# One gather for both expert tables in a hybrid decoder step: 8 KB rows, eight places, weights made column by column

## The chip, the cores and the metric

One core of one Trainium2 chip runs the whole program. The metric is the device time in microseconds. The kernel before took 2368.91 us, the median of three runs (2366.36 to 2372.15). Engines are named as in the profile: PE is TensorE (PEld its weight loads), DVE VectorE, ACT ScalarE, POOL GpSimd, SP SyncE; a "q" behind a name is the engine's sequencer.

## The reference

One layer of a decoder, for 512 prompt tokens and 8 x 8 sample tokens with a paged past of 2048. Two attention mixers (one over selected keys, one over a compressed latent) are projected and added to x; then comes the part that the change touches, a feed-forward layer of 16384 single-neuron experts, of which each token takes 16 for each of 8 heads:

```python
# PEER, for a block of 128 tokens xb (normalised)
q = (xb @ w_peer_q).reshape(128, 8, 2, 64)
s = einsum('thpd,hpnd->thpn', q, peer_sub_keys)       # two halves, 128 keys each
sv, si = top_k(s, 16)
cand = sv[:, :, 0, :, None] + sv[:, :, 1, None, :]    # 256 pairs per head
cv, ci = top_k(cand, 16)                              # e: the expert of each pair
g = softmax(cv)
act = gelu(einsum('td,thkd->thk', xb, peer_u[e]))
y = einsum('thk,thkd->td', g * act, peer_v[e])        # added to x1
```

Both tables, peer_u and peer_v, are 16384 x 1024 in float32: one row is 4 KB.

## The kernel before

The program has one long prelude (to about 441 us: projections of five tiles of 128 tokens, prompt attention, routing of the first tile) and then a loop of steps (line 1072 on ACT, 1679 on DVE, 2217 on PE). All engines run the same steps by number, each in its own instruction stream, tied only by semaphores.

A column is one expert for each of 128 tokens, one token per partition. There are 128 columns for each of four prompt tiles and 64 for the sample tile, 576 in all. POOL gathers a column's rows by an indirect DMA with 128 indices (line 682): one from peer_u and one from peer_v, 512 KB each. The row of peer_u for column k is fetched for step k; that of peer_v for step k + LAG with LAG = 22. A ring of 16 places of 4 KB per partition takes both kinds in the order of use, and now and then a chunk of query weights or output weights ("w", "o"). POOL fills a place when the one who used it last is done: the dot for a row of peer_u, the transposes or the addition for a row of peer_v, the matmuls for a weight chunk.

At step k DVE multiplies the landed row of peer_u by the token's vector h (kept in PSUM, h_now) and sums it into acts[column] (line 1690, the dot). After 16 columns ACT applies gelu to all 16 sums (line 1078) and DVE multiplies by the gates into wts (line 1706). The row of peer_v is taken in one of two ways, by the list SHARES (line 342), which names for stretches of steps the share that goes to DVE: either ACT scales the row by its weight in place (line 1086) and PE one step later adds it to accT in PSUM by eight transposes against the identity (line 2230); or DVE multiplies and adds it into xall (line 1701). The sample tile's columns all go the first way. When a tile is over, ACT copies the sums out of PSUM and PE turns them back.

Between these column parts each engine's step has other parts, put down by a plan of first and last step and a count of marks (lines 362 to 389): eight batches of latent attention (b0 to b7, 55 steps each from step 36), the indexer's scores (idx, 100 to 160), the search for the selected keys by 32 trials (top, 166 to 351), eight batches of attention over selected keys (a0 to a7, from 361), the routing of the next tile (r1 to r4: norm, query matmuls, key scores) and the choice of its experts (c1 to c4), and the second half of the first tile's choice (c0b, 0 to 36). The pages of the caches are gathered on the same POOL queue (line 623), at places in the order of fetches that AHEAD sets. The norm of tile t puts its row into hbuf (line 1236), from which PE turns it and DVE copies it to h_now. mix_rest (line 1407) adds the output projection of the last two prompt tiles at step MIXED_AT = LAG; PE's first transposes and the first latent batch wait for it. Eight of the 16 places are the space of w_out and come free as the projection uses it.

## Time and profile before

| what | value |
|---|---|
| median of three runs | 2368.91 us (2366.36 to 2372.15) |
| span of the profiled execution | 2346.3 us (22.6 us below the median; its own total time isn't shown) |
| PE, PEld busy | 1763.5 us (75%), 1299.5 us (55%) |
| DVE busy | 1610.7 us (69%) |
| ACT busy | 989.6 us (42%) |
| POOL busy | 1234.0 us (53%) |
| HBM read, written | 690.14 MB, 3.76 MB |
| gathers of peer_u, peer_v (line 682) | 576, 576 |
| granted PE clock, mean | 0.807 |

The span is the time from the first to the last instruction of one profiled execution. Busy shares are averages over all stages. Issue time of a DMA on POOL counts as busy; the transfer does not. A wait names the engine whose semaphore came last by the profile; "issue" means that nothing in the profile explains the pause, and "another core or an unknown queue" (in the waits: remote) an event without an engine.

### The profile page before, as it was taken

The page shows a single profiled execution, that of the slowest core. Times are in us where ns is not written, and L with a number is a line of the kernel's source. Part 1 is how long each engine was busy: PE and PEld are TensorE (multiplying, and loading weights), DVE is VectorE, ACT ScalarE, POOL GpSimd, SP SyncE. Part 2 cuts the span into 40 slices and gives each one's busy share as a digit, 9 for nine tenths or more (in the row PEclk, how much of TensorE's full clock was granted, in tenths as well). Part 3 has the DMA queues.
Part 4 walks back from the last instruction along what each step waited for, and adds up shares of the span by engine and source line. Part 5 has one row for each costly group of instructions (what it writes and reads, how often), then busy time and mean ns, then how long its engine had stood idle before and what let it go on. Part 6 is the DMA issues. An engine that isn't in the chain of part 4 may idle for free.

```text
span 2346.3 us, 26214 instructions
## 1 busy us (share of the span) xinstructions
PE 1763.5 (75%) x8918; PEld 1299.5 (55%) x8918; DVE 1610.7 (69%) x3641; ACT 989.6 (42%) x1711; POOL 1234.0 (53%) x1251
## 2 busy tenths in 40 slices
PE   7995999638858967987877977847876976753556
PEld 3553657327646756665655755636654655543445
DVE  2546682887876777778676786786887778677441
ACT  1223343133544323555665664643342443233345
POOL 1000000367666666666667666656566656767664
PEclk9997799858977857978978987977987887875667
DMA  7001202499998989999999999979899889999997
GB/s 256 24 11 38 56 1 73 156 354 405 351 342 331 346 312 353 354 359 370 344 361 392 372 354 385 344 262 389 314 354 376 314 325 348 373 401 348 358 372 283
DMA packets 191573, 695.64 MB, mean 296 GB/s; under 512 B 26192, under 2 KB 28624, under 8 KB 188368
## 3 DMA queue, kind: packets, MB, share of 16 engines
q0 software_dynamic: 178608, 674.33, 76.2%
q1 hardware_dynamic: 12832, 19.65, 2.8%
q8 instruction: 70, 1.15, 0.2%
q14 instruction: 63, 0.52, 0.1%
HBM read 690.14 MB, written 3.76 MB: 296 GB/s over the span
## 4 chain that ended last, share of the span: by engine, by line
PE 42%; DVE 21%; issue 12%; POOL 6%; ACT 6%; another core or an unknown queue 5%; DVEq 4%; DMA 4%; ACTq 0%; POOLq 0%
PE ps L2230 8%; PE ps L2037 7%; DVE region L1690 6%; POOL region L682 6%; DVEq L1097 4%; DVE xall L1701 3%; DMA region<-in_peer_v,region 3%; PE ps L1722 2%; ACT region L1086 2%; PE ps L2054 2%; PE ps L1987 2%; PE ps L2130 1%; PE ps L2019 1%; PE ps L2082 1%
## 5 line engine op out<-in xcount | busy, mean ns | idle before, releaser
L682 POOL DMA_INDIRECT region<-in_peer_u,region x507 | 515.7, 1017 | 611.6 <-DVEq L1097 440.1
L2230 PE MATMUL ps<-ident,region 128*128 128x128 f32 x3312 | 552.7, 325 | 262.4 <-issue 138.1
L682 POOL DMA_INDIRECT region<-in_peer_v,region x571 | 571.7, 1001 | 335.2 <-issue 145.8
L1690 DVE SCALAR_TENSOR_TENSOR region<-region,h_now 128x1024 f32<-128x1024 f32 x507 | 611.7, 1214 | 116.5 <-DMA region<-in_peer_u,region 69.6
L2230 PEld LDWEIGHTS ps<-ident,region 128*128 128x128 f32 x3312 | 472.1, 169 | 350.6 <-issue 204.3
L1086 ACT ACTIVATE region<-region 128x1024 f32<-128x1024 f32 x414 | 464.9, 1139 | 245.0 <-DMA region<-in_peer_v,region 189.0
L2037 PE MATMUL ps<-w_uk_s,region 128*128 128x512 f32 x544 | 294.3, 669 | 8.7 <-issue 6.7
L1701 DVE SCALAR_TENSOR_TENSOR xall<-region,xall 128x1024 f32<-128x1024 f32 x157 | 201.7, 1285 | 20.9 <-issue 4.7
L2037 PEld LDWEIGHTS ps<-w_uk_s,region 128*128 128x128 f32 x544 | 106.3, 218 | 91.8 <-issue 88.2
L946 ACT ACTIVATE region<-ps 128x512 f32<-128x512 f32 x136 | 80.2, 590 | 163.5 <-PE ps L2037 101.3
L953 ACT ACTIVATE region<-ps 128x256 f32<-128x256 f32 x136 | 51.5, 379 | 202.2 <-remote 115.0
L1428 DVE TENSOR_REDUCE region<-region 128x8 f32<-128x512 f32 x136 | 92.6, 681 | 62.4 <-issue 41.2
L1690 DVE SCALAR_TENSOR_TENSOR tables<-tables,h_now 128x1024 f32<-128x1024 f32 x69 | 83.9, 1216 | 21.6 <-DMA tables<-in_peer_u,region 16.6
L682 POOL DMA_INDIRECT tables<-in_peer_u,region x69 | 70.8, 1026 | 29.6 <-issue 18.9
L2017 PE MATMUL ps<-region 128*128 128x64 f32 x272 | 52.5, 278 | 43.1 <-issue 29.2
L2017 PEld LDWEIGHTS ps<-region 128*128 128x128 f32 x272 | 47.4, 209 | 67.3 <-issue 50.1
L2054 PE MATMUL ps<-region 128*64 128x256 f32 x272 | 72.9, 424 | 8.9 <-issue 4.7
L2130 PE MATMUL ps<-region 128*128 128x64 f32 x272 | 51.2, 346 | 37.4 <-ACT region L1033 20.9
L2130 PEld LDWEIGHTS ps<-region 128*128 128x128 f32 x272 | 47.1, 256 | 50.6 <-issue 25.3
L1722 PE MATMUL ps<-region 128*128 128x512 f32 (+1 forms) x192 | 69.3, 515 | 5.5 <-ACT region L703 5.5
L864 ACT ACTIVATE region<-region,stat 128x128 f32<-128x128 f32 (+3 forms) x64 | 35.9, 561 | 81.5 <-DVE stat L1368 81.4
L1003 ACT ACTIVATE region<-region 64x2056 bf16<-64x2056 f32 x32 | 63.8, 1994 | 0.0
(404 smaller groups left out, 2824.5 us busy)
## 6 DMA issues: line engine op xcount, KB each, us to landing
region<-in_w_peer_q POOLq DMA_DIRECT2D x31, 512.0 KB
region<-in_peer_v,region POOLq DMA_INDIRECT x571
region<-in_peer_u,region POOLq DMA_INDIRECT x507
region<-in_w_in POOLq DMA_DIRECT2D x8, 882.0 KB, 14.8
region<-in_w_peer_q SPq DMA_DIRECT2D x8, 512.0 KB, 4.7
region<-in_x_turned SPq DMA_DIRECT2D x5, 512.0 KB, 3.5
region<-in_w_out SPq DMA_DIRECT2D x2, 1024.0 KB, 12.4
region<-in_w_out SPq DMA_DIRECT2D x1, 2048.0 KB, 18.3
```

What stands on the lines that cost most here:

```text
L682: pool.indirect_dma_start(ring[r][:], None, table, bass.IndirectOffsetOnAxis(ap=experts[:, t, n:n + 1], axis=0)).then_inc(landed[r], 16)
L1086: sc(ring[r][:], ring[r][:], ACT.Copy, scale=wts[:, t % 2, n:n + 1]).then_inc(S["v_scaled"], 1)
L1097: dve.drain()
L1428: v.tensor_reduce(norm_s[:, q - 3, :], sq_s[:, n % 2, :].rearrange("p (h d) -> p h d", h=HB), AX, ALU.add).then_inc(S["reduced"], 1)
L1690: v.scalar_tensor_tensor(ring[r][:], ring[r][:], 1.0, h_now[:], ALU.mult, ALU.mult, accum_out=acts[:, t % 2, n:n + 1]).then_inc(S["u_done" ...
L1701: v.scalar_tensor_tensor(xall[:, t, :], ring[r][:], wts[:, t % 2, n:n + 1], xall[:, t, :], ALU.mult, ALU.add).then_inc(S["v_mixed"], 1)
L1722: last = te.matmul(ps[2 + i][:, 0:w], xT[:, t % 2, c, :], w_in[:, c, c0:c0 + w], start=(c == 0), stop=(c == KD - 1))
L2017: te.matmul(dst, cT_s[:, m % 2, 0, :], qabs[:, 0, :, cols], start=True, stop=False)
L2037: last = te.matmul(ps[2][:], cT_s[:, m % 2, c, :], w_uk[:, c, :], start=(c == 0), stop=(c == 1))
L2054: te.matmul(ps[2][0:NTOK, 0:DC], s_s[:, g, :], c_s[:, g, :], start=(g == 0), stop=(g == NPG))
L2130: last = te.matmul(ps[5][:, g % 8 * NTOK:(g % 8 + 1) * NTOK], kT_s[:, (q - 1) % 2, g - g0, :], q_blk[:], start=True, stop=True)
L2230: last = te.matmul(ps[6 + c // 4][:, (c % 4) * P:(c % 4 + 1) * P], ring[r][:, c * P:(c + 1) * P], ident[:], is_transpose=True, start=(m == ...
```

## The change

The host lays both tables side by side as one array peer_rows of 16384 x 2048, so that an expert's rows are one row of 8 KB. One gather per column brings it. The ring has eight places of 8 KB: three in the space of the former first six, four in that of w_out, and the last over hbuf and the space behind it, free after the first dot. The normalised row of tiles 1 to 4 therefore goes to tables (h_rows) instead of hbuf. Two weight chunks share a place. The lag of 22 steps goes: at step k DVE does the dot of column k; ACT, for column k - 1, applies gelu to the one sum, multiplies by the gate with a copy, and scales the second half of the row where PE takes it; DVE's addition is for column k - 1 and waits for ACT's weight; PE's transposes are for column k - 2. A place is free when the row has been added. The first columns (steps below 6) and the first four columns of tiles 1 to 3 go to DVE; the list's last entry goes. MIXED_AT is 6. Per column ACT gets two small activations and one or two drains; the grouped gelu on ACT and the grouped product on DVE go.

```diff
-        ring = [Region(X_END + r * D, KEPT_END).view(D) for r in range(EXTRA)]
-        ring.append(tables[:, 0:D])
-        ring.append(Region(HBUF_AT + D, SIZE).view(D))
-        ring += [Region(W_OUT_PLACE + c * D, W_OUT_PLACE + KD * D).view(D) for c in range(KD)]
-        W_OUT_AT = EXTRA + 2
+        W = 2 * D
+        ring = [Region(X_END + r * W, X_END + EXTRA * D).view(W) for r in range(EXTRA // 2)]
+        W_OUT_AT = len(ring)
+        ring += [Region(W_OUT_PLACE + c * W, W_OUT_PLACE + KD * D).view(W) for c in range(KD // 2)]
+        HBUF_SLOT = len(ring)
+        ring.append(Region(HBUF_AT, SIZE).view(W))
+        h_rows = [hbuf] + [tables[:, 0:D]] * (NTILE - 1)
...
-        LAG = 22
-        GRP = 16
+        ADD_LAG, PE_LAG = 1, 2
-        SHARES = [(38, 54, 3, 4), (100, 160, 2, 3), (167, 184, 1, 2), (258, 275, 1, 2), (362, 480, 3, 5), (480, 496, 1, 2), (SEQ, STEPS, 1, 2)]
+        MIXED_AT = 6
+        SHARES = [(0, MIXED_AT, 1, 1), (38, 54, 3, 4), (100, 160, 2, 3), (167, 184, 1, 2), (258, 275, 1, 2), (362, 480, 3, 5), (480, 496, 1, 2)]
+        HEAD = 4
         def on_dve(m):
-            k = m + LAG
+            if P <= m < SEQ and m % P < HEAD:
+                return True
+            k = m + ADD_LAG
...
-        AHEAD = NRING // 2 - 1
+        AHEAD = NRING - 1
...
-            if k < NCOLS:
-                fetched.append(("u", *tile_of(k)))
-            if k >= LAG:
-                fetched.append(("v", *tile_of(k - LAG)))
+            fetched.append(("e", *tile_of(k)))
...
-                    if kind_ == "u":
-                        pool.wait_ge(S["u_done"], x + 1)
-                    elif kind_ != "v":
+                    if kind_ != "e":
                         pool.wait_ge(S["w_used"], weights_used(fetched[f - NRING]))
                     elif on_dve(x):
                         pool.wait_ge(S["v_mixed"], x - pe_rows(x) + 1)
                     else:
                         pool.wait_ge(S["v_added"], pe_rows(x) + 1)
+                elif f == HBUF_SLOT:
+                    pool.wait_ge(S["dotted"], 1)
                 elif f >= W_OUT_AT:
-                    pool.wait_ge(S["o_up"], 4 + f - W_OUT_AT + 1)
+                    pool.wait_ge(S["o_up"], 4 + 2 * (f - W_OUT_AT) + 2)
...
-                    table = a["peer_u"] if kind == "u" else a["peer_v"]
-                    pool.indirect_dma_start(ring[r][:], None, table, ...)
+                    pool.indirect_dma_start(ring[r][:], None, a["peer_rows"], ...)
...
-                if k % GRP == 1 and 1 < k <= NCOLS + 1:
-                    j = k // GRP - 1
-                    act.wait_ge(S["dotted"], j + 1)
-                    t, n = tile_of(GRP * j)
-                    sc(acts[:, t % 2, n:n + GRP], acts[:, t % 2, n:n + GRP], ACT.Gelu_apprx_tanh).then_inc(S["gelu"], 1)
+                m = k - ADD_LAG
                 if 0 <= m < NCOLS:
-                    if m % GRP == 0:
-                        act.wait_ge(S["wts"], m // GRP + 1)
+                    act_, weight = acts[:, t % 2, n:n + 1], wts[:, t % 2, n:n + 1]
+                    act.wait_ge(S["dotted"], m + 1)
+                    sc(act_, act_, ACT.Gelu_apprx_tanh)
+                    act.drain()
+                    sc(weight, act_, ACT.Copy, scale=gates[:, t, n:n + 1]).then_inc(S["wts"], 1)
                     if not on_dve(m):
-                        act.wait_ge(landed[r], landing["v", t, n])
-                        sc(ring[r][:], ring[r][:], ACT.Copy, scale=wts[:, t % 2, n:n + 1]).then_inc(S["v_scaled"], 1)
+                        act.drain()
+                        sc(ring[r][:, D:W], ring[r][:, D:W], ACT.Copy, scale=weight).then_inc(S["v_scaled"], 1)
...
-                    v.scalar_tensor_tensor(ring[r][:], ring[r][:], 1.0, h_now[:], ALU.mult, ALU.mult,
-                                           accum_out=acts[:, t % 2, n:n + 1]).then_inc(S["u_done"], 1)
-                    if k % GRP == GRP - 1:
-                        settle()
-                        dve.sem_inc(S["dotted"], 1)
-                m = k - LAG
+                    v.scalar_tensor_tensor(ring[r][:, 0:D], ring[r][:, 0:D], 1.0, h_now[:], ALU.mult, ALU.mult,
+                                           accum_out=acts[:, t % 2, n:n + 1]).then_inc(S["dotted"], 1)
+                m = k - ADD_LAG
                 if 0 <= m < NCOLS and on_dve(m):
-                    dve.wait_ge(landed[r], landing["v", t, n])
+                    dve.wait_ge(S["wts"], m + 1)
                     settle()
-                    v.scalar_tensor_tensor(xall[:, t, :], ring[r][:], wts[...], xall[:, t, :], ALU.mult, ALU.add).then_inc(S["v_mixed"], 1)
-                if k % GRP == 2 and 2 < k <= NCOLS + 2:
-                    dve.wait_ge(S["gelu"], j + 1)
-                    v.tensor_tensor(wts[:, t % 2, n:n + GRP], acts[:, t % 2, n:n + GRP], gates[:, t, n:n + GRP], ALU.mult).then_inc(S["wts"], 1)
+                    v.scalar_tensor_tensor(xall[:, t, :], ring[r][:, D:W], wts[...], xall[:, t, :], ALU.mult, ALU.add).then_inc(S["v_mixed"], 1)
...
-                m = k - LAG - 1
+                m = k - PE_LAG
```

## Rows read from the trace of the kernel before

**Rows 1.** Busy us (instructions) by stretch, granted PE clock, DMA share, GB/s
```profile
441.00:586.00 145.00, 91.36 (x455) 67.01 (x454) 114.60 (x265) 42.48 (x71) 99.21 (x103) 0.77 0.95 368
586.00:735.00 149.00, 109.15 (x567) 79.88 (x568) 116.19 (x337) 72.36 (x108) 95.27 (x98) 0.80 0.95 355
735.00:952.00 217.00, 177.71 (x898) 136.02 (x898) 159.93 (x223) 73.52 (x159) 138.62 (x134) 0.74 0.90 328
952.00:1541.00 589.00, 476.43 (x2670) 358.32 (x2668) 433.99 (x1076) 362.01 (x552) 387.56 (x400) 0.87 0.97 364
1541.00:2006.00 465.00, 340.91 (x1786) 260.61 (x1786) 361.05 (x498) 166.26 (x312) 290.73 (x278) 0.78 0.88 333
2006.00:2124.00 118.00, 74.35 (x415) 61.50 (x413) 86.21 (x213) 42.89 (x54) 78.15 (x84) 0.77 0.97 377
2124.00:2346.00 222.00, 115.91 (x618) 96.93 (x616) 95.36 (x150) 88.71 (x83) 137.69 (x144) 0.65 0.92 349
```

**Rows 2.** Timeline of POOL in the end stretch: start us, us, instruction, idle before
```profile
2223.30 0.94 POOL L682 DMA_INDIRECT region<-in_peer_v,region  x1 [0.30 <-issue]
```

**Rows 3.** Stretches of line 1690 (twice), line 1086, line 1701 alone
```profile
586.00:2124.00 1538.00, 554.42 (x916) 0.81 0.93 350
952.00:1541.00 589.00, 231.37 (x382) 0.87 0.97 364
...
586.00:2124.00 1538.00, 359.98 (x322) 0.81 0.93 350
...
586.00:2124.00 1538.00, 174.75 (x136) 0.81 0.93 350
```

**Rows 4.** Stretches as in rows 1, with 4 KB rows, then 8 KB rows
```profile
2222.00:2232.00 10.00, 6.28 (x25) 5.07 (x26) 4.92 (x8) 4.29 (x5) 6.56 (x7) 0.50 1.03 413
1697.50:1699.50 2.00, 2.00 (x16) 1.60 (x14) 2.00 (x3) 0.94 (x3) 1.70 (x2) 1.00 0.98 399
```

**Rows 5.** Chain of waits by line, of 586 to 2124, then 2124 to 2346
```profile
by line: issue 13.2%; PE ps L2037 10.3%; PE ps L2230 9.8%; DVE region L1690 7.2%; another core or an unknown queue 5.3%; DVEq L1097 4.5%; DVE xall L1701 3.9%; PE ps L2054 3.2%; ACT region L1086 3.1%; DMA region<-in_peer_v,region 2.7%; PE ps
by line: POOL region L682 43.3%; issue 19.7%; PE ps L2230 14.1%; another core or an unknown queue 8.5%; DMA region<-in_peer_v,region 4.8%; POOL tables L682 3.0%; DVE region L1690 1.1%; ACT region L1086 1.0%; DVE xall L1701 0.6%; DVE h_now L
```

**Rows 6.** Waits of 586 to 2124: us in total, times, longest
```profile
ACT region L1086 <- DMA region<-in_peer_v,region: 80.3, 30, 9.0
POOL region L682 <- remote: 79.5, 45, 3.8
PEld ps L2230 <- ACT region L1086: 77.1, 50, 16.1
POOL region L682 <- PE ps L2230: 76.9, 45, 4.7
```

**Rows 7.** Line 623, gathers of 8 KB rows: ns min/median/max, first and last start
```profile
L623 POOL DMA_INDIRECT region<-in_cache_a_v,page_idx x8: 932/936/1790, 1583.5 to 1951.8; - x8
```

**Rows 8.** Timeline of DVE (last dot) and of PE at the end
```profile
2299.95 1.22 DVE L1690 SCALAR_TENSOR_TENSOR region<-region,h_now 128x1024 f32<-128x1024 f32 x1 [1.32 <-DMA region<-in_peer_u,region]
...
2337.42 1.04 PE L2230 MATMUL ps<-ident,region 128*128 128x128 f32 x8
```

**Rows 9.** Timeline of DVE at the first landed row
```profile
446.05 1.23 DVE L1688 COPY h_now<-region 128x1024 f32<-128x1024 f32 x1 [4.05 <-DMA region<-in_peer_u,region]
```

**Rows 10.** Groups of instructions on ACT: busy us, mean ns
```profile
L836 ACT ACTIVATE stat<-stat 128x1 f32<-128x1 f32 x5 | 1.0, 203 | 0.1
```

**Rows 11.** Timeline of ACT around a grouped gelu
```profile
1313.63 1.28 ACT L1078 ACT_TABLE_LOAD   x1
1314.93 0.22 ACT L1078 ACTIVATE region<-region 128x16 f32<-128x16 f32 x1
1315.05 1.13 ACT L1086 ACTIVATE region<-region 128x1024 f32<-128x1024 f32 x1
```

**Rows 12.** Groups of table loads on ACT, first and last of six lines
```profile
L1078 ACT ACT_TABLE_LOAD x24 | 30.8, 1283 | 0.4
...
L932 ACT ACT_TABLE_LOAD x5 | 6.4, 1283 | 0.1
```

More of the change, by code:

```diff
@@ L364, in program @@
         C_PAGES = [(0, 6), (6, 12), (12, NPG + 1)]
-        chain_b = [(f"b{b}", 36 + 55 * b, 36 + 55 * b + 50, MB) for b in range(NB)]
-        MIXED_AT = LAG
+        B_AT = 36
+        chain_b = [(f"b{b}", B_AT + 55 * b, B_AT + 55 * b + 50, MB) for b in range(NB)]
         NBIT = 31
@@ L399, in program @@
             for c, k in enumerate(marks(f"r{t}", 6, KD)):
-                weights[k].append(("w", t, c))
+                if c % 2 == 0:
+                    weights[k].append(("w", t, c))
         for c, k in enumerate(marks("mixS", 0, KD)):
-            weights[k].append(("o", NTILE - 1, c))
-        AHEAD = NRING // 2 - 1
+            if c % 2 == 0:
+                weights[k].append(("o", NTILE - 1, c))
+        AHEAD = NRING - 1
         pages = [[] for _ in range(STEPS)]
-        pages[MIXED_AT + AHEAD].append(("b", 0))
+        pages[B_AT - NRING + AHEAD].append(("b", 0))
         pages[88].extend((("i", 0), ("i", 1)))
@@ L415, in program @@
         fetched, beside = [], {}
-        for k in range(NCOLS + LAG):
+        for k in range(NCOLS):
             beside[len(fetched)] = pages[k]
             fetched += weights[k]
-            if k < NCOLS:
-                fetched.append(("u", *tile_of(k)))
-            if k >= LAG:
-                fetched.append(("v", *tile_of(k - LAG)))
-        assert sum(len(x) for x in weights[NCOLS + LAG:] + pages[NCOLS + LAG:]) == 0
+            fetched.append(("e", *tile_of(k)))
+        assert sum(len(x) for x in weights[NCOLS:] + pages[NCOLS:]) == 0
         place_of, landing, count = {}, {}, [0] * NRING
@@ L426, in program @@
             r = f % NRING
[L427 removed]
+            count[r] += 2 * KVA * 16 if what[0] == "o" and what[2] < G else 16
             place_of[what], landing[what] = r, count[r]
         def weights_used(what):
[L432 removed]
+            return KD * ((NTILE if what[1] == NTILE - 1 and what[0] == "w" else what[1])) + what[2] + 2
         def advance(k, parts):
@@ L1983, in route @@
                 for c in range(KD):
-                    r = place_of["w", t, c]
-                    pe.wait_ge(landed[r], landing["w", t, c])
+                    r = place_of["w", t, c // 2 * 2]
+                    pe.wait_ge(landed[r], landing["w", t, c // 2 * 2])
                     for h in range(PH):
-                        last = te.matmul(ps[3 + 2 * (h // 4)][:, (h % 4) * P:(h % 4 + 1) * P], ring[r][:, h * P:(h + 1) * P], h2T[:, c, :],
+                        last = te.matmul(ps[3 + 2 * (h // 4)][:, (h % 4) * P:(h % 4 + 1) * P], ring[r][:, c % 2 * D + h * P:c % 2 * D + (h + 1) * P], h2T[:, c, :],
                                          start=(c == 0 and h % 4 == 0), stop=(c == KD - 1), skip_group_check=True)
@@ L2181, in mix_sample @@
                 for c in range(KD):
-                    r = place_of["o", NTILE - 1, c]
-                    pe.wait_ge(landed[r], landing["o", NTILE - 1, c])
+                    r = place_of["o", NTILE - 1, c // 2 * 2]
+                    pe.wait_ge(landed[r], landing["o", NTILE - 1, c // 2 * 2])
                     for j, bank in enumerate((3, 5)):
-                        last = te.matmul(ps[bank][:], oT_s[:, c, :], ring[r][:, 512 * j:512 * j + 512], start=(c == 0), stop=(c == KD - 1))
+                        x = c % 2 * D + 512 * j
+                        last = te.matmul(ps[bank][:], oT_s[:, c, :], ring[r][:, x:x + 512], start=(c == 0), stop=(c == KD - 1))
                     last.then_inc(S["w_used"], 1)
@@ L2281 @@
     for name in _INS:
-        arrays[name] = _np.ascontiguousarray(inputs[name])
+        if name not in ("peer_u", "peer_v"):
+            arrays[name] = _np.ascontiguousarray(inputs[name])
+    arrays["peer_rows"] = _np.concatenate([inputs["peer_u"], inputs["peer_v"]], axis=1)
     arrays["page_table"] = _np.ascontiguousarray(_np.repeat(arrays["page_table"].T, P // NPG, axis=0))
```

51 lines of the change are left out of this document (25 added, 26 removed).

## Prediction

> **What bounds the kernel now.** I read the stretches of the span first, then the chain of waits, then the waits themselves. The rows of experts are fetched from 441 us to the end, 1905 of the 2346.3 us. [rows 1] cuts that into the start (441 to 586), five stretches that I call the middle (586 to 2124, in which other work goes with the columns: sample attention, routing, the top-key search), and the end (2124 to 2346, hardly anything but columns). The reader should see that no engine is full in the middle. Summed over its five rows PE is busy 1178 of 1538 us (77%), DVE 1157 (75%), ACT 717 (47%), POOL 990 (64%). But POOL's 994 instructions each stand 0.30 us apart although nothing holds them [rows 2], so its queue is occupied 990 + 298 = 1288 us, 84%. The DMA engines show 0.93 [rows 3], and moved 350 GB/s there; with nothing in the way they reached 413 in [rows 4], so bytes alone want 350/413 = 85% of the middle. So five resources stand at 75 to 85%, and the loss is in waiting for one another.
>
> The chain of waits says who waits last [rows 5]. In the end stretch it is POOL issue: 43.3 + 3.0% on line 682. Two gathers a column at 0.94 + 0.30 us [rows 2] are 2.49 us, beside 1.049 MB at 413 GB/s = 2.54 us of transfer: two bounds of one size, so that after any hiccup neither can catch up, and 64 columns took 222 us with their tail. In the middle the chain is PE first, then DVE; landings (DMA 2.7%, unknown queue 5.3%, which I read as gathers landing, the only work I know without an engine's name) are 8% of 1538 = 123 us. The waits agree: ACT's scaling waited 80 us for rows of the second table, POOL 80 + 77 us for free places [rows 6].
>
> **The change part by part.** Sums are against the profiled execution, whose own total time is not shown; its span is 2346.3 us, 22.6 under the median of 2368.91. I take that as constant and state differences.
>
> *Half the gathers, rows twice as long.* 1152 gathers become 576. A gather with 8 KB rows already stands in the trace (the value cache) and costs POOL a median 0.936 us [rows 7], as one of 4 KB does. POOL's load per column falls from 2.49 to 1.24 us. The bytes stay. A burst of 8 KB rows ran 399 GB/s at a DMA share of 0.98, 4 KB rows 413 at 1.03 [rows 4]: 407 against 401 per unit of share. I take the rate per byte as equal (2.54 us a column); bounds are 2.50 and 2.63 (1.049 MB at 399).
>
> *End, without the lag of 22.* 64 columns at 2.6 us (2.54 and little for stalls) are 166 us. After the last landing come one dot (554.4/458 = 1.21 us [rows 3]), gelu and weight (0.6, below), scaling (1.12 [rows 3]), eight transposes (1.04), and then what follows them today, from 2338.5 to 2346.3 [rows 8]: 12 us. 178 against 222: **-44**. Bounds -50 (2.5 us a column) and -20 (2.97, 353 GB/s, near the middle's rate).
>
> *Start, without the lag.* The first 54 columns now need both tables' rows, where before the second ran 22 columns behind. 54 x 1.049 + 4.2 (query weights) + 2.4 MB (pages) = 63.2 MB at 413 GB/s = 153 us, and 4 us until the first landing [rows 9]: 157, and 3 more because only three places are free at once and four await the output projection. 160 against 145: **+15**. Bounds +5 (routing work hidden less now) and +27 (at the start's 368 GB/s it would be 172).
>
> *Middle, relief.* POOL at half load refills a stall at twice the transfer's rate. Of the 123 us of landings on the chain I take 60%, since PE, DVE or ACT is next to be late: **-75**. Bounds 0 (others are late at once) and -151 (all of it and some 28 us of POOL issue that lies in shorter stretches of the same chain).
>
> *Middle, ScalarE's load.* Instead of one gelu over 16 columns there is, in every column, a gelu of 128x1, a drain, a copy with a pointer scale, and for PE columns a second drain before the scaling. The nearest row, an activation of 128x1, takes 203 ns [rows 10]; the copy I put at 0.25. Today the scaling starts 0.12 us after a gelu of 0.22 began [rows 11], an overlap of 0.10 that two drains take away: 0.20 + 0.25 + 2 x 0.10 = 0.65, less the share of the old gelu (0.22/16), say 0.6 us a column. Bounds 0.45 and 0.9. ACT goes from 362 to 362 + 0.6 x 191 columns [rows 3] = 477 of 589 us (81%) in the stretch 952 to 1541, from 61%: it becomes as full as PE. Where PE sat waiting for a scaling, 50 times in the middle [rows 6], I add the 0.6 in full: **+30**. Bounds 0 and 193 (all 322 scaled columns [rows 3]).
>
> *Middle, VectorE's addition.* An addition (136 in the middle [rows 3]) waited only for a landed row; now it waits for ACT's weight of the column before. ACT sits first behind its own parts of the step before, which wait for PE. The dot of 1.21 us in front covers 0.6 us if ACT is free. Behind the waiting addition stand DVE's parts and the next dot, and behind those PE. I take 0.25 us each, +34; bounds 0 and 136 x 0.8 = 109 (a square of 0.6 and a copy left over on ACT). The additions themselves go from 159 to 157 by the shares: nothing.
>
> *Table loads.* Gelu, Exp and Sqrt take each other's table out. 24 loads for gelu and 32 for the others (8 + 8 + 6 + 5 + 5, of six lines the first and the last in [rows 12]) stand in the trace, of which all but one or two are in this phase. Afterwards each of the 33 Exp and Sqrt there (two for each of eight latent-attention batches, one for each of eight selected-key batches, four norms, five gates) has one before and one after: at most 66, some 12 more x 1.283 = 15 us of ACT, a third of it on the path: **+5**, bounds 0 and 15.
> The trace has ACT going on 0.02 us after a load ended [rows 11]. The Trainium skill (ScalarE: Activation LUTs, What ACT_TABLE_LOAD costs) says that a switch also drains for about 1.38 us, 2.66 in total, and speaks against a gelu in every column. By it the 12 would cost 32 us of ACT and the term would be +11; by the row it is +5, and no row here shows that drain.
>
> *Places.* Eight places of 8 KB hold as many columns as sixteen of 4 KB. A row now keeps its place through dot, gelu, scaling and transposes, about 5 us or 1.5 steps longer than the first table's did. About 5 columns (13 us of transfer) stay ahead. I cost that at nothing while stalls are under 13 us; the page gathers profit a little, as POOL comes to them later and waits less.
>
> Sum: -44 + 15 - 75 + 30 + 34 + 5 = **-35 us, 2334 us**.
>
> **The rivals.** *B, supply was the bound all along.* For it: POOL 84% and DMA 0.93 in the middle, and 13% of the chain as issue, some of which may be landings. Against: PE and DVE lines lead the chain. All of the 151 goes and the additions' waits shrink to 10: -44 + 15 - 151 + 30 + 10 + 5 = -135, 2234 us.
>
> *C, slower: dot, gelu, scaling and transposes become one chain that every step walks.* Place: ACT in the middle. Price 0.6 us for each column in which ACT is the last. For it: ACT at 81% from 952 to 1541, and DVE, ACT and PE now tied within one or two steps, where today ACT may run ahead of the dots by half a group. Against: today's waits of PE for a scaling are only 50. The rest of the sum is -44 + 15 - 75 + 34 + 5 = -65, so it decides from 65/0.6 = 108 columns on; at 200 of the 322 the time is 2369 - 65 + 120 = 2424 us.
>
> *D, bytes bound it.* The DMA share stays as it is, every added wait hides behind transfer, and the middle does not move. End at its own 373 GB/s (64 columns 180 us, + 12) gives -30, start at 377 (168 + 4) gives +27: 2366 us. For it the share of 0.93 to 0.97; against it 413 GB/s in [rows 4] with 4 KB rows.
> The Trainium skill (DMA: Bandwidth & Descriptors, Specifications) gives an HBM limit of about 358 GB/s per core, by which the middle's 350 would leave nothing to win and D would hold; the trace's 413 over 10 us disagrees, and the measurement decides.
>
> **How the numbers follow.** Forecast A (2300 to 2361) 0.34, B 0.22, C 0.33, D 0.11. No change means within 0.3%, 7 us, about what a measurement of this kernel can tell. Faster: A and B, 0.56; same: D, 0.11; slower: C, 0.33. The range takes in B's middle and C's up to its worked case: 2235 to 2430. A's own is 2300 to 2361.
>
> **What would show it.** POOL busy falls to about 650 us with gathers still at 0.94; if they take 1.5 or more, the first step is wrong. Columns in the end stretch come every 2.5 to 2.6 us. From the start of the last dot to the end of the span it is 12 us, today 46 [rows 8]. ACT's busy time rises by 200 to 300 us. DVE's additions wait for ACT where they waited for nothing. ACT_TABLE_LOADs are 60 to 70. If PE's waits for the scaling line grow from 50 to over 150 and the stretch of the key search is longer than now, C holds. If that stretch shrinks by over 5%, B does. The forecast is wrong in its largest term if the middle still waits for landings as before.

## Result and profile after

The changed kernel takes 2189.18 us (median, 2181.62 to 2195.00), the kernel before beside it 2370.07 (2366.36 to 2372.15): ratio 0.9233 [0.921, 0.9256], 181 us faster. I had forecast 2334 in a range of 2235 to 2430, so the direction was right and the size far off. The nearest rival was B (supply was the bound all along), 2234.

The profiled execution took 2195.0 us with a span of 2193.2. Only 1.8 us lie around the span, so the 22.6 us that I took as constant were no fixed part of a run: the profiled execution of before was itself some 20 us quicker than its median. From trace to trace the gain is 153 us; some 22 of the other 28 are that, and the rest is that this execution of the changed kernel lay 6 us above its median.

Three stretches of the changed kernel, cut at the same columns as in [rows 1] (dots 54 and 512 start at 613 and 2018); columns as there:

```profile
441.00:613.00 172.00, 130.96 (x634) 93.88 (x632) 127.12 (x276) 88.24 (x196) 63.16 (x66) 0.82 0.94 384
613.00:2018.00 1405.00, 1115.97 (x6246) 846.74 (x6246) 1155.80 (x2321) 933.51 (x2068) 508.12 (x516) 0.85 0.96 382
2018.00:2193.00 175.00, 115.02 (x555) 92.95 (x553) 81.91 (x134) 111.09 (x203) 56.26 (x61) 0.65 0.92 379
```

| stretch | before | after | moved | my sum |
|---|---|---|---|---|
| start | 145 (441 to 586) | 172 | +27 | +15 |
| middle | 1538 | 1405 | -133 | -6 (-75 + 30 + 34 + 5) |
| end | 222 | 175 | -47 | -44 |

The middle is where the forecast broke. PE and DVE do the same work there as before, PE for fewer us because its granted clock rose from 0.81 to 0.85 (1116 us against the 1178 summed from [rows 1]). The DMA engines moved 382 GB/s instead of 350, at a share of 0.96 instead of 0.93.

From the changed kernel's page, engine totals and groups (busy us, mean ns, idle time before and who ended most of it):

```profile
PE 1738.6 (79%) x8934; PEld 1272.8 (58%) x8934; DVE 1601.9 (73%) x3603; ACT 1273.8 (58%) x2840; POOL 634.3 (29%) x657
...
q0 software_dynamic: 95376, 674.29, 76.7%
...
L689 POOL DMA_INDIRECT region<-in_peer_rows,region x576 | 567.2, 985 | 1421.5 <-PE ps L2229 752.9
...
L1091 ACT ACTIVATE region<-region 128x1024 f32<-128x1024 f32 x419 | 481.3, 1149 | 34.5 <-issue 0.8
L1086 ACT ACTIVATE region<-region 128x1 f32<-128x1 f32 x576 | 113.2, 196 | 330.3 <-DVE region L1696 322.6
...
L1704 DVE SCALAR_TENSOR_TENSOR xall<-region,xall 128x1024 f32<-128x1024 f32 x157 | 201.8, 1285 | 78.1 <-ACT region L1088 64.0
L1088 ACT ACTIVATE region<-region 128x1 f32<-128x1 f32 x576 | 169.7, 295 | 40.1 <-issue 0.7
```

The reader should see POOL at 634 us (1234 before) with the gather of 8 KB rows at a mean of 985 ns, and on ACT 576 gelus of 0.196 and 576 copies of 0.295 us. ACT's total rose from 989.6 to 1273.8. POOL idles 753 us for PE's transposes: it waits for places, no longer the other way round. The same bytes went in 95,376 packets; the page of before has 178,608.

Waits of the changed kernel in its middle (us in total, times, longest), then its chain of waits by line in the middle and in the end stretch:

```profile
POOL region L689 <- PE ps L2229: 612.3, 255, 19.5
ACT region L1086 <- DVE region L1696: 221.3, 134, 6.1
PEld ps L2229 <- ACT region L1091: 191.5, 134, 7.1
...
DVE region L1696 <- DMA region<-in_peer_rows,region: 78.6, 63, 6.4
...
DVE xall L1704 <- ACT region L1088: 60.7, 35, 5.2
```

```profile
by line: DVE region L1696 12.3%; PE ps L2035 9.0%; PE ps L2229 7.4%; DMA region<-in_peer_rows,region 6.4%; DVE xall L1704 6.0%; ACTq L1087 5.9%; DVEq L1103 4.4%; issue 4.0%; PE ps L1985 3.0%; PE ps L2052 2.7%; ACT region L1091 2.7%; ACT reg
```

```profile
by line: DMA region<-in_peer_rows,region 66.4%; PE ps L2229 8.9%; DVE region L1696 5.7%; ACT region L1091 4.7%; issue 3.7%; POOL region L689 3.2%; ACT region L1088 1.3%; PE ps L2204 1.1%; ACT region L1076 1.0%; ACT region L1086 0.9%; anothe
```

Against [rows 5], "issue" fell from 13.2 to 4.0% and the unknown queue is gone from the front places; the dot, PE's latent attention and the additions lead. Landings are 6.4%, 90 us. PE's weight loads wait for a scaling 134 times (191 us) where [rows 6] has 50 (77 us). In the end stretch landings, 66.4%, have taken POOL's place.

### The profile page after: what moved, and what is told of

It reads as the page before. It is cut to its first block, busy times and chain, and to the rows that moved or that the text cites. A ratio compares the mean times of both kernels' runs of the same rounds, so it can differ in the third digit from the quotient of the medians.

```text
span 2193.2 us, 27671 instructions
## 1 busy us (share of the span) xinstructions
PE 1738.6 (79%) x8934; PEld 1272.8 (58%) x8934; DVE 1601.9 (73%) x3603; ACT 1273.8 (58%) x2840; POOL 634.3 (29%) x657
## 3 DMA queue, kind: packets, MB, share of 16 engines
q0 software_dynamic: 95376, 674.29, 76.7%
## 4 chain that ended last, share of the span: by engine, by line
PE 38%; DVE 28%; DMA 12%; ACT 9%; ACTq 4%; DVEq 4%; issue 4%; POOL 1%; another core or an unknown queue 0%; POOLq 0%
DMA region<-in_peer_rows,region 11%; DVE region L1696 9%; PE ps L2035 6%; PE ps L2229 6%; DVE xall L1704 4%; DVEq L1103 4%; ACTq L1087 4%; PE ps L1985 3%; PE ps L1720 3%; ACT region L1091 2%; PE ps L2052 2%; ACT region L1088 1%; PE ps L2017 1%; PE ps L1888 1%; ACT region L1010 1%
## 5 line engine op out<-in xcount | busy, mean ns | idle before, releaser
L689 POOL DMA_INDIRECT region<-in_peer_rows,region x576 | 567.2, 985 | 1421.5 <-PE ps L2229 752.9
L1696 DVE SCALAR_TENSOR_TENSOR region<-region,h_now 128x1024 f32<-128x1024 f32 x576 | 695.8, 1216 | 203.4 <-DMA region<-in_peer_rows,region 191.1
L2229 PE MATMUL ps<-ident,region 128*128 128x128 f32 x3352 | 567.8, 327 | 248.0 <-ACT region L1091 225.1
L1091 ACT ACTIVATE region<-region 128x1024 f32<-128x1024 f32 x419 | 481.3, 1149 | 34.5 <-issue 0.8
L1086 ACT ACTIVATE region<-region 128x1 f32<-128x1 f32 x576 | 113.2, 196 | 330.3 <-DVE region L1696 322.6
L2035 PE MATMUL ps<-w_uk_s,region 128*128 128x512 f32 x544 | 282.1, 644 | 5.9 <-ACT region L953 5.9
L1088 ACT ACTIVATE region<-region 128x1 f32<-128x1 f32 x576 | 169.7, 295 | 40.1 <-issue 0.7
L1985 PEld LDWEIGHTS ps<-region 128*128 128x128 f32 x512 | 61.3, 197 | 5.6 <-issue 3.8
L1985 PE MATMUL ps<-region 128*128 128x128 f32 x512 | 62.7, 280 | 1.2 <-ACT region L905 1.2
L1947 PE MATMUL ps<-ident,region 128*128 128x128 f32 x160 | 34.4, 318 | 36.6 <-ACT region L871 36.3
L2017 PE MATMUL ps<-region 32*128 32x64 f32 x272 | 61.2, 306 | 0.0
L2015 PEld LDWEIGHTS ps<-region 128*128 128x128 f32 x272 | 46.6, 205 | 24.4 <-issue 13.9
```

The source lines that it names most:

```text
L689: pool.indirect_dma_start(ring[r][:], None, a["peer_rows"], bass.IndirectOffsetOnAxis(ap=experts[:, t, n:n + 1], axis=0)).then_inc(landed[ ...
L1086: sc(act_, act_, ACT.Gelu_apprx_tanh)
L1088: sc(weight, act_, ACT.Copy, scale=gates[:, t, n:n + 1]).then_inc(S["wts"], 1)
L1091: sc(ring[r][:, D:W], ring[r][:, D:W], ACT.Copy, scale=weight).then_inc(S["v_scaled"], 1)
L1696: v.scalar_tensor_tensor(ring[r][:, 0:D], ring[r][:, 0:D], 1.0, h_now[:], ALU.mult, ALU.mult, accum_out=acts[:, t % 2, n:n + 1]).then_inc( ...
L1985: last = te.matmul(ps[3 + 2 * (h // 4)][:, (h % 4) * P:(h % 4 + 1) * P], ring[r][:, c % 2 * D + h * P:c % 2 * D + (h + 1) * P], h2T[:, c, ...
```

## Experiments

All times are medians. Sets of executions on different chips differ for the kernel before (2340 to 2373, and one of 2137, below), hardly for the changed one, so I compare changed kernels with each other, and on one chip where 10 us matter. Kernels with two gathers may move with the chip as the kernel before does, and none was run on two chips, so a difference of 10 us between two of them tells nothing. The changed kernel beside later variants took 2185.45.

> The changed kernel itself, beside the other three on one chip, so that differences of ten microseconds can be told: 2185 to 2195.

Its trace has the first dot at 446 and dot 54 at 604, where the first trace had 455 and 613: 9 of the start's +27 us belong to that one execution.

**Two gathers, everything else changed.** The two tables stay apart, and each column takes two gathers of 4 KB rows into the halves of one place:

```diff
-  pool.indirect_dma_start(ring[r][:], None, a["peer_rows"], ...)
+  for half, table in ((ring[r][:, 0:D], a["peer_u"]), (ring[r][:, D:W], a["peer_v"])):
+      pool.indirect_dma_start(half, None, table, ...)
```

> The changed kernel, with each column's two rows fetched again by two gathers of 4 KB rows from the two tables into the two halves of the same place. Lag, places, gelu per column stay as changed. Theory S (the supply held the middle: two gathers a column on POOL at 1.24 us each and the shorter rows): most of the 181 us come back, 2330 to 2390 us, POOL's queue over 80% occupied again, columns of the end stretch back at 2.5 us or more. Rival L (the gain came from what goes with it: no lag, other shares, places freed otherwise): it stays at 2190 to 2230.

Measured: 2340.98, ratio 0.9939 [0.9901, 0.9977] to before. Its stretches:

```profile
448.00:625.00 177.00, 128.15 (x602) 95.73 (x601) 119.83 (x262) 87.21 (x196) 114.63 (x119) 0.72 0.97 370
625.00:2146.00 1521.00, 1160.07 (x6242) 872.25 (x6241) 1157.68 (x2321) 934.33 (x2068) 979.39 (x971) 0.82 0.95 352
2146.00:2341.00 195.00, 118.71 (x558) 96.99 (x556) 81.88 (x134) 110.57 (x203) 115.80 (x124) 0.61 0.91 341
```

The whole gain but 14 us is gone. The one gather is worth 152 us by the medians; by the traces it is 116 in the middle, 19 in the start (177 against the changed kernel's 158, both from the first dot to dot 54), 20 in the end. The stretch of the key search, steps 184 to 351, is back at 521 us (518 before, 470 changed). And the middle is 17 us shorter than before's 1538 although all of ACT's new work and the additions' waits are in it: whatever they cost while supply binds, the rest of the change gave more. PE's busy time is 1160 us in the middle at a clock of 0.82, 44 more than in the changed kernel for the same work. The chain of waits in this middle:

```profile
by line: issue 11.3%; DVE region L1697 8.4%; PE ps L2036 8.0%; PE ps L2230 7.4%; another core or an unknown queue 5.6%; DVE xall L1705 5.5%; ACT region L1092 4.1%; POOL region L690 4.1%; ACTq L1088 4.1%; DVEq L1104 2.9%; DMA region<-in_peer
```

"Issue" at 11.3% and the unknown queue at 5.6% come back with the second gather alone, so both go with supply.

**Without gelu and weights, with one gather and with two.** Gelu and the product with the gate are left out; rows are scaled by the gate alone.

```diff
-  sc(act_, act_, ACT.Gelu_apprx_tanh)
-  act.drain()
-  sc(weight, act_, ACT.Copy, scale=gates[:, t, n:n + 1]).then_inc(S["wts"], 1)
   if not on_dve(m):
-      act.drain()
-      sc(ring[r][:, D:W], ring[r][:, D:W], ACT.Copy, scale=weight)...
+      sc(ring[r][:, D:W], ring[r][:, D:W], ACT.Copy, scale=gates[:, t, n:n + 1])...
```

> The changed kernel without the gelu, its drain and the copy that makes the weight: ACT scales the row, and DVE adds it, by the gate alone (left out: gelu and the product with the dot). The order to the dot is kept on ACT. The prediction charged this work and the wait of DVE's additions 30 + 34 + 5 = 69 us in the middle: by that the kernel takes 2110 to 2135 us. Rival H (the work lies beside waits for transfer): 2175 to 2195. If ACT was on every column's path (the prediction's case C), under 2060.

> Two gathers of 4 KB per column as in the variant that took 2341, and gelu and the product with the gate left out (rows are scaled by the gate alone). With one gather, leaving this out gave 56 us. If supply bounds the kernel with two gathers, ACT's added work is hidden there and leaving it out gives under 15 us: 2326 to 2341. If the two costs add up, as my sum had it, it gives the same 56 again: 2275 to 2295.

Measured: 2133.88 with one gather (55 less than with the chain), 2318.88 with two (22 less, or some 15 when each is taken against the kernel before beside it, 2347 and 2355). Their middles, one gather first:

```profile
607.00:1958.00 1351.00, 1099.20 (x6258) 841.66 (x6257) 1156.07 (x2320) 672.72 (x1111) 508.14 (x517) 0.85 0.98 398
```

```profile
614.00:2112.00 1498.00, 1158.10 (x6282) 876.52 (x6282) 1159.15 (x2318) 670.61 (x1119) 986.80 (x978) 0.82 0.96 359
```

| middle, us | with gelu and weights | without |
|---|---|---|
| two gathers | 1521 | 1498 |
| one gather | 1405 | 1351 |

(The second window lies 7 us ahead of dots 54 and 512 of its kernel; from dot to dot it is 1497.) The chain costs 54 us in the middle with one gather, 23 with two. I had priced it at 30 + 34 + 5 = 69. But these variants leave out more than the change had added: ACT's busy time in the middle falls to 673 us, under the 717 of the kernel before, and its table loads from 73 to 25, where the kernel before has 62. So 54 us is more likely too high than too low for the new work alone. Most of it is owed only once supply has stopped binding. With two gathers the saving by the medians is at or over the 15 us that I had set for "hidden" and far under 55: mostly hidden, not wholly.

**Half the bytes.** One gather of the first table's 4 KB rows alone; the second table's rows are left out.

> The changed kernel, gathering only the first table's 4 KB of each column (left out: the second table's rows; what lies in the place is scaled and added). One gather a column, half the bytes. It shows what is left when transfer no longer binds. If the DMA engines still bound the changed kernel everywhere (0.96 of the middle), it falls far, to 1800 to 1950 us. If the engines' own chain is next at once, it stays over 2100. The end stretch should go from 2.56 us a column to about 2 (dot, gelu, scaling chain on ACT 1.7 us).

Measured: 2105.36. Its middle:

```profile
588.00:1981.00 1393.00, 1114.75 (x6246) 848.72 (x6246) 1153.71 (x2321) 932.72 (x2068) 511.47 (x516) 0.85 0.65 212
```

At 212 GB/s it is 12 us shorter than the changed kernel's 1405: after the change the engines' own chain binds the middle, and bytes hardly at all. Start and end do shrink, from 158 to 138 (from the first dot) and from 175 to 125; those two follow the transfer.

**What of the second gather costs: POOL's time?** A first filler of four drains and memsets missed its size.

```diff
   pool.indirect_dma_start(ring[r][:], None, a["peer_rows"], ...)
+  for _ in range(4):
+      pool.drain()
+      pool.memset(tables[:, D:D + 112], 0.0)
```

> The changed kernel, with one gather of 8 KB rows a column as changed, and behind each gather four pairs of a drain and a memset of 128x112 on POOL, in columns of a table that nobody reads any more. It loads POOL's queue about as the second gather did, without packets. If POOL's occupancy was the supply's bound (theory S, POOL part) it is slow like the kernel with two gathers, 2300 to 2390 us. If the shorter packets of the DMA engines were the larger part, it stays under 2230. Between them the share of each can be read, with the memsets' measured time.

Measured: 5004.57. Its timeline of POOL (start, us, instruction, idle before) shows why:

```profile
1509.36 1.12 POOL L693 MEMSET tables<- 128x112 f32 x4 [4.62 <-issue]
1510.97 1.71 POOL L690 DMA_INDIRECT region<-in_peer_rows,region  x1 [0.49 <-issue]
```

The first memset starts 4.6 us after the gather before it ended, at its neighbours 6.3 and 7.0 (over all 576 gathers 4.5 to 10.9, median 4.7): the drain behind a gather stood still that long. So this kernel says nothing on my question. Fillers without a drain, ahead of the gather, do:

```diff
+  if k_fill:
+      pool.wait_ge(S["filled"], k_fill)
+  for i in range(NFILL):                       # 4, 16, 32
+      pool.memset(tables[:, D + w * i:D + w * i + w], 0.0).then_inc(S["filled"], 1)   # w = 28, 7, 3
+  k_fill += NFILL
   pool.indirect_dma_start(ring[r][:], None, a["peer_rows"], ...)
```

> The changed kernel with four memsets of 128x28 on POOL ahead of every gather of rows, so that POOL is held about as long per column as by a second gather (an estimate of 1.1 to 1.3 us more), while the transfers stay one row of 8 KB. If POOL's time is what the second gather cost, the 152 us between 2341 (two gathers of 4 KB) and 2189 come back for the most part: 2300 to 2350. If the longer rows themselves are what helps (fewer, longer packets; one landing instead of two), the time stays within 25 us of the changed kernel: 2189 to 2215. Between them, the share that comes back is POOL's share.

> The changed kernel with sixteen memsets of 128x7 on POOL ahead of every gather of rows: by the four that held it 0.43 us, this is 1.2 to 1.7 us more per column, a POOL queue as full as with two gathers, with packets of 8 KB. POOL's time as the cause: 2310 to 2345, and more than that if the memsets hold it over 1.25 us. Length of packets as the cause: under 2215.

> The changed kernel with thirty-two memsets of 128x3 on POOL ahead of every gather of rows; sixteen of 128x7 held POOL 0.76 us per column and cost 14 us. With 1.3 to 1.5 us of memsets POOL is held 2.5 to 2.7 us per column, as long as by two gathers or longer. If POOL's queue is the price of the second gather: 2310 to 2360. If the packets of 4 KB carry most of it (in the start stretch, at a DMA share of 1.00, 389 GB/s against 418, 7% of some 1700 us), POOL's part is the rest, 20 to 50 us: 2205 to 2240.

Measured: 2192.86, 2199.47 (14 over the changed kernel on the same chip) and 2223.12. POOL in the last one:

```profile
1202.00 1.05 POOL L694 MEMSET tables<- 128x3 f32 x32
1203.20 0.94 POOL L696 DMA_INDIRECT region<-in_peer_rows,region  x1 [0.15 <-POOL tables L694]
1204.15 1.05 POOL L694 MEMSET tables<- 128x3 f32 x32
```

From memset to memset it is 2.15 us where nothing holds POOL up, less than I had expected. With four and with sixteen memsets the shortest steps are 1.4 and 1.7 us. So POOL's time per column prices as: 1.24 us, nothing; 1.4, 4 to 7 us; 1.7, 14; 2.15, 34 to 38 (2223 against 2185 to 2189). Two gathers hold it 2.49. This curve bends up as POOL comes nearer to the transfer's 2.5 us, and explains some 36 us of the 152 and perhaps more; I have no point at 2.49 with 8 KB rows. The memsets stand behind POOL's wait for a place, so each gather also starts 1.2 us after its place is free, as the second of a pair does; the 36 us hold both effects.

**Or the packets?** Two gathers of 64 rows of 8 KB were to keep the packets and double the gathers.

```diff
+  for p0 in (0, 64):
+      pool.indirect_dma_start(ring[r][p0:p0 + 64, :], None, a["peer_rows"], ... experts[0:64, ...])
```

> The changed kernel with two gathers per column, each of 64 rows of 8 KB into one half of the place's partitions (the second half takes the experts of tokens 0 to 63 of the neighbouring column, so tokens 64 on are computed from other rows). The number of gathers is that of the variant with two gathers of 4 KB rows (2341), the packets are those of one gather (2189). If POOL's time per gather is what a second gather costs (0.94 + 0.30 us whatever its rows), the time is 2310 to 2345. If the length of the rows is what the change brings, it is 2185 to 2210. If a gather of 64 rows holds POOL for half as long, this doesn't tell them apart, and POOL's busy time in the profile will say so.

Measured: 3217.94 (3174.95 to 4108.23, four executions), outside both expectations. Its middle:

```profile
719.00:2931.00 2212.00, 1343.35 (x6255) 986.93 (x6253) 1174.51 (x2320) 950.79 (x2069) 901.42 (x978) 0.71 1.01 244
```

The DMA engines are never idle (1.01) and move 244 GB/s. Rows that go into half the partitions land at little over half the rate, and the question stayed open. So three bursts were appended behind the last column, with nothing reading them:

> The changed kernel with three bursts of 64 columns' gathers appended on POOL when the columns are done, with nothing reading them: pairs of 128 rows of 4 KB, single gathers of 128 rows of 8 KB, pairs of 64 rows of 8 KB. The output stands as it is; only the time of each burst counts. 64 columns are 67.1 MB. If the rate per byte is the same for both lengths, as I had it, the first two bursts take the same 161 us (417 GB/s), or the first is held by POOL at 64 x 2.49 = 159. If 4 KB packets are slower at full DMA share, the first takes 170 to 175 us (389 GB/s) against 161. The third tells whether rows into half the partitions are slow by themselves: by the variant that had them, 229 to 250 GB/s, 268 to 293 us; else 161.

> The three bursts once more, on another chip. On the chip where the kernel before took 2137 us, 64 columns took 171 us as pairs of 4 KB rows (POOL at its 1.24 us per gather, no packet over 172 ns) and 165 us as 8 KB rows. If the kernel before takes 2330 to 2373 us beside this run and its 4 KB packets are slow by themselves there, the first burst takes 178 to 190 us and the second still 165. If the first burst stays at 171, packets of 4 KB are no slower by themselves, and what costs on such a chip comes only with the other work or with waiting.

Measured, total 2820.97 and 2824.99, one execution each. From first issue to the next burst's, 64 columns took 170.9 and 170.7 us as pairs of 4 KB rows, 164.6 and 164.0 as single 8 KB rows. The windows of the second run, in the same order with the pairs of 64 rows last:

```profile
2195.00:2335.00 140.00, 0.00 (x0) 0.00 (x0) 0.00 (x0) 0.00 (x0) 105.51 (x114) 0.50 1.03 410
2365.00:2500.00 135.00, 0.00 (x0) 0.00 (x0) 0.00 (x0) 0.00 (x0) 48.47 (x52) 0.50 1.01 420
2530.00:2790.00 260.00, 0.00 (x0) 0.00 (x0) 0.00 (x0) 0.00 (x0) 101.31 (x114) 0.50 1.02 220
```

4 KB rows go at 410 GB/s by themselves, POOL keeping 1.24 us per gather, against 420. That is 0.105 us a column, 60 us over 576 if these rates held in the kernel. "Equal rate per byte", which I read from 10 us and 2 us in [rows 4], was off by 2.5% in a burst. In the middles it is 352 against 382 GB/s at DMA shares of 0.95 and 0.96, so the engines are not idle for longer: their packets take longer per byte. In the packet records a packet of 4 KB lasted 163 ns on average in the bursts (99% at most 172) and one of 8 KB 315; in the middles it is 176 with two gathers (the longest 1% over 630) and 327 in the changed kernel, 8% apart per byte. The long packets of 4 KB come almost only beside the kernel's other work. Whether they are a cause of the lost time or go with it, no run shows.

**Places and lags.**

```diff
-  ring.append(Region(HBUF_AT, SIZE).view(W))   # seven places
-  ADD_LAG, PE_LAG = 1, 2
+  ADD_LAG, PE_LAG = 2, 3                       # or 2, 2
```

> The changed kernel with seven places instead of eight. If stalls of the engines are longer than what lies ahead (I cost the places at nothing while stalls are under 13 us), a place less costs in proportion: 15 to 50 us, 2205 to 2240. If places are no limit: within 10 us of 2189.

> The changed kernel with the lags of addition and of transposes behind the dot one step longer (2 and 3 instead of 1 and 2). If the waits dot to gelu to scaling to transposes are what bounds the middle now, a step of slack takes away most of DVE's wait for a weight (61 us in the middle) and part of PE's wait for a scaling (149): 20 to 60 us faster, 2130 to 2170. If places are what is short, each is held 2.5 us longer, and the time is the same or up to 40 us longer: 2189 to 2230.

> Lags 2 and 3 beside the changed kernel on one chip: 2179 was measured on another chip than the changed kernel's 2189. If the step of slack is worth anything, it is faster by 5 to 15 us here too; if that was the chip, within 4 us of it.

> The changed kernel with the addition (and with it gelu and scaling) two steps behind the dot and the transposes also two. It tells what the 9 us of lags 2 and 3 come from: if from gelu no longer waiting for the dot (ACT's waits for the dot fell from 215 to 116 us in the middle), it stays at 2175 to 2182; if from PE's step of slack, it falls back to 2189 or above, up to 2230 as PE now meets the scaling in its own step.

> Lags 2 and 3, and between steps 362 and 480 half of the columns on DVE instead of three fifths (twelve additions of 1.28 us less on DVE, twelve scalings and sets of transposes more). Half the bytes left these stretches at 370 and 113 us, so the engines bind there: if it is DVE, 5 to 12 us faster than 2178; if it is PE, 5 to 15 us slower.

Measured: seven places 2216.81, the middle 1431 us, 26 longer. Lags 2 and 3: 2179.22, and 2177.94 beside the changed kernel's 2185.45 on one chip, so 7.5 us faster (2176.02 to 2184.37 against 2181.21 to 2191.83, four executions each); the traces have 7 us of it in the middle. Lags 2 and 2: 2336.19, far over both expectations: PE now meets the scaling in its own step, and its waits for it grow (below). Lags 2 and 3 with fewer columns on DVE: 2177.58, no further gain or loss, where I had expected one or the other. Waits of lags 2, 3 and then of lags 2, 2, in the middle:

```profile
POOL region L689 <- DVE xall L1704: 178.4, 77, 7.1
PEld ps L2229 <- ACT region L1091: 163.3, 114, 8.1
...
DVE region L1696 <- DMA region<-in_peer_rows,region: 115.9, 81, 6.8
ACT region L1086 <- DVE region L1696: 110.6, 68, 5.1
```

```profile
PEld ps L2229 <- ACT region L1091: 353.3, 203, 8.5
PE ps L2229 <- ACT region L1091: 291.5, 168, 8.2
```

A step of slack halves ACT's waits for the dot (221 to 111 us) but gives most of it back in places: POOL waits 178 us instead of 114 for additions, DVE 116 instead of 79 for landings. Lags 2 and 3 are the best changed version run.

**The kernel before on another chip.** Beside the bursts' first run and its three neighbours the kernel before took 2137.14 (seven executions, 2132.78 to 2143.84). Beside every other set it took 2345 to 2373.

> The kernel before, profiled once more. Beside the last four kernels, on a chip that had not been used till then, it took 2137 us (7 executions within 11), where four other sets of executions had it at 2347 to 2373, while the changed kernel's variants stood at the same times on all chips. If this chip is like the first four: 2340 to 2375, with a DMA share of 1.0 and 370 to 390 GB/s in its end stretch. If it is like the last: about 2137, and its trace says in which stretches the 210 us are and whether the packets of 4 KB are shorter there.

Measured: 2340.00 (2331.24 to 2369.78), on yet another chip. The trace is of an execution that took 2365.76; its middle is 18 us longer than the first one's 1538 and otherwise like it:

```profile
446.00:585.00 139.00, 85.59 (x433) 64.42 (x433) 112.78 (x260) 40.56 (x66) 93.56 (x98) 0.74 0.96 374
585.00:2141.00 1556.00, 1174.98 (x6342) 893.68 (x6340) 1157.52 (x2345) 719.00 (x1186) 984.86 (x992) 0.82 0.92 346
2141.00:2364.00 223.00, 119.66 (x616) 98.67 (x616) 95.45 (x150) 88.82 (x83) 137.22 (x144) 0.63 0.92 347
```

So I have no trace of the kernel before at 2137. On that chip the changed kernel with lags 2 and 3 and fewer columns on DVE took 2177.58, the same as on the others (2178, 2179), ratio 1.0192 [1.016, 1.0223]: 40 us slower than before. The changed kernel itself wasn't timed there; from its distance of 7.5 us to its variant it would be near 2186, some 50 us slower than before. The first run of the bursts, on that chip too, bears this out: from the first dot to the last its columns took 1726 us, against 1724 in the second trace of the changed kernel. The bursts of 4 KB rows took 171 us there and 171 on a chip where the kernel before took 2364, so gathers of 4 KB rows by themselves are no quicker on it, and POOL issues them at the same 1.24 us. The filler of thirty-two memsets was timed on that chip as well, and its 2223 us are 37 over this 2186. So POOL's time per gather is not what sets the chips apart. The kernel before had a granted clock of 0.84 there, 0.80 to 0.82 elsewhere; whether that comes from shorter waits or brings them is open, and so is the cause.

## Why the prediction was wrong

- **Half the gathers (right).** 576 gathers at a median 0.936 us, POOL busy 634 us; I had said 0.94 and about 650.
- **End, -44 (right, -47).** 64 columns and tail take 175 us, 178 forecast. After the last dot starts 13.7 us pass, 12 forecast and 46.3 before. The last dot of the changed kernel:

```profile
2179.51 1.22 DVE L1696 SCALAR_TENSOR_TENSOR region<-region,h_now 128x1024 f32<-128x1024 f32 x1 [1.26 <-DMA region<-in_peer_rows,region]
```

- **Start, +15 (right in size).** +27 in this execution, +18 in the second.
- **ScalarE's load +30, additions' waits +34, table loads +5 (sum rather too high, and wrongly added).** ACT rose by 284 us (forecast 200 to 300), table loads on the six lines of my count came to 67 (56 before, 60 to 70 forecast). Without gelu and weights the middle is 54 us shorter with one gather, and that leaves out more than the change added, so 69 was too high by 15 us or more. Additions waited for a weight 61 us in the middle, where I had 34; the split between the terms was not tested, only their sum.
- **Middle, relief -75: the step that failed.** I read supply's part from the chain of waits as the 123 us of landings in [rows 5], and took 60% of it. The runs give 116 us for the middle with the chain in, 147 without it (1498 to 1351). And most of the 69 us of costs that I set against it were not yet owed while supply bound: with two gathers and all of the costs the middle was 17 us shorter than before. So this step failed twice: the term was mis-sized, and it was added to costs that it had first to free.
- **How the miss divides.** The miss of 127 us in the middle (-133 against -6) is 41 of relief (116 against 75) and 86 of the rest of the change (-17 against +69). Since 23 of the costs are paid even with two gathers, something else in the change, which I had at nothing, seems to have given back about as much and 17 us more: the lag, the places or the shares. No run takes these apart, and the two traces of the kernel before differ by 18 us in the middle. The two errors fit one root, which the runs support but don't prove: I added terms as if each stood on the path, while in [rows 1] POOL's queue at 84% and transfers at a share of 0.93 bound much of the middle together, and PE and DVE, leading the chain, were often only the last to be held up by them. "Issue" at 13.2% of the chain was the row that I gave to rival B alone: it is 11.3% with two gathers and everything else changed, and 4.0% with one.
- **Rival B** named that cause and its signs held: steps 184 to 351 (the key search) went from 518 to 470 us, 9% less. Its -151 was meant for the middle, where the gather was worth 116 or 147; that the gather gave 152 over the whole span is a coincidence. The +45 that it set against this did not come either (-17), so its -106 lay near -133 in part because two errors offset each other. It missed 45 us: 28 lie between trace and median (above), 27 in the middle (-133, B's terms for it made -106), less 9 in start and end.
- **Rival C** had the right mechanism for after the change, not the size: half the bytes save only 12 us in the middle. PE's loads wait for a scaling 134 times, under the 150 that I had set.
- **Rival D** is out: bytes were as many, and the middle moved.
- **Places, at nothing.** Seven places cost 26 us in the middle, so one place less costs; eight are probably a small limit too, as POOL's waits for a place suggest, but no run had nine.

On one chip the sum without its relief term, +40, is near what was seen, some 40 to 50 us slower; there is no trace of the kernel before there to say whether for that reason. On the others the kernel before loses 203 to 236 us more, and the change takes that away with the costs in it. What stays open: how the 152 us divide. The memsets put POOL's time at some 36. The rates of the bursts put 4 KB rows at 60; the rates in the middles, 352/0.95 = 371 against 382/0.96 = 398 GB/s per unit of share, would by an estimate be 7% of 0.95 x 1521, or 100 us in the middle alone, if transfer were always the limit. These overlap, PE's lower clock may carry a part of its own, and no run separates them, nor says why one chip doesn't pay.

## What to carry over

Before adding up costs and gains, ask whether one resource holds all stages up: costs on other engines are mostly hidden until it is relieved, and then owed together. Two feeds at 84 and 93% were such a resource here, even if the chain of waits shows compute in front; test it by halving one of them alone. Time the kernel before on more than one chip when the change is about supply.

## What the hardware showed unexpectedly

- Rows into 64 partitions moved at 220 to 224 GB/s in a burst, into 128 at 420, though such gathers came in pairs that covered both halves. The gather of 64 rows held POOL 0.89 us, that of 128 rows 0.94. The Trainium skill (SBUF — State Buffer, Door 1: The DMA port swizzle) says that the top bit of the partition number picks one of two ports in each cluster, so that partitions 0 to 63, or 64 to 127, reach half of the ports; the measured half rate agrees.
- A drain on POOL behind a gather waited 4.5 to 10.9 us before the next instruction, median 4.7.
- Per byte, packets of 4 KB took 3.5% longer than packets of 8 KB in bursts (163 against 315 ns), 8% longer in the middles of the kernels (176 against 327).
- On ACT an activation of 128x1 took 0.196 us, a copy of 128x1 with a scale from memory 0.295 ([rows 10] had 0.203 for another).
- Sixteen memsets of 128x7 took 0.61 us, thirty-two of 128x3 1.04 us: 33 to 38 ns each.
- The kernel before took 2137 us on one chip and 2340 to 2373 on the others; the changed kernel (2189 and 2185) and its variant with lags 2 and 3 (2179 and 2178), on two chips each, differed by under 0.3%.
